# Two-block transformer kernel: the order of gate units around the first attention, and the place of one spread gate row

## The reference

```python
mod = c @ w_ada[l] + b_ada[l]
h = rmsnorm(x, norm_g[l]) * (1.0 + scale[:, None]) + shift[:, None]
qkv, z_attn, u_pool, z_pool, g_attn, g_pool = split(h @ w_in[l])
attn = sum_over_groups(softmax(lse) * attention(q, k, v, dilation, bias))
y_attn = (attn * silu(z_attn)) @ w_attn_br[l]
y_pool = (mixed_pool * silu(z_pool)) @ w_pool_br[l]
merged = sigmoid(g_attn) * y_attn + sigmoid(g_pool) * y_pool
x = x + gate[:, None] * (merged @ w_out[l])
```

```python
x = sublayer_residual(x, y, g1, ln_g[i, 0], ln_b[i, 0])
x = sublayer_residual(x, sq_relu_mlp(x * (1.0 + sc2) + sh2, w1[i], w2[i]), g2, ln_g[i, 1], ln_b[i, 1])
```

## Time and profile before

| | us |
|---|---|
| median of 3 runs | 1415.87 |
| lowest and highest | 1415.29, 1424.77 |
| the profiled execution | 1417.43 |
| its span in the profile | 1415.7 |
| PE busy | 1319.8 (93%) |
| DVE busy | 845.3 (60%) |
| ACT busy | 578.3 (41%) |
| POOL busy | 163.6 (12%) |

### The profile page before, as it was taken

How to read it: one execution, slowest core, us unless ns; L and a number is a source line. 1 busy time by engine, 2 the same in 40 slices (tenths; PEclk the granted TensorE clock), 3 DMA queues, 4 the chain that set the end, 5 groups by cost and what they waited for, 6 DMA issues and landing times.

```text
span 1415.7 us, 24506 instructions
## 1 busy us (share of the span) xinstructions
PE 1319.8 (93%) x10521; PEld 1216.9 (86%) x10521; DVE 845.3 (60%) x1265; ACT 578.3 (41%) x889; POOL 163.6 (12%) x167
## 2 busy tenths in 40 slices
PE   5999999999998999888999999999999998899995
PEld 2899988899887778778989898998999997899995
DVE  1867655565454355538765556655679875556663
ACT  2533345635753434414422313213254663434440
POOL 0111100000011111015400000000030121100002
PEclk8999999999999999999999999999999998899998
DMA  9987874545244543335444444434236003345550
GB/s 350 324 296 243 261 224 109 149 152 177 79 151 159 179 162 108 117 117 184 142 156 129 152 138 147 151 106 150 75 119 206 4 1 120 115 153 179 181 176 30
DMA packets 163593, 218.40 MB, mean 154 GB/s; under 512 B 5998, under 2 KB 141557, under 8 KB 163350
## 3 DMA queue, kind: packets, MB, share of 16 engines
q1 hardware_dynamic: 141060, 152.30, 32.8%
q0 software_dynamic: 21728, 63.23, 14.2%
q10 hardware_dynamic: 698, 1.32, 0.3%
HBM read 215.70 MB, written 1.12 MB: 153 GB/s over the span
## 4 chain that ended last, share of the span: by engine, by line
PE 76%; DVE 10%; ACT 5%; DMA 4%; issue 3%; POOL 1%; POOLq 0%; SPq 0%; DVEq 0%; ACTq 0%
PE bank L1301 29%; PE bank L701 11%; PE bank L718 10%; PE bank L751 6%; DVE wlo L2024 2%; PE bank L1377 2%; PE bank L812 2%; PE bank L734 2%; DMA graw_b<-in_w_mod 2%; DVE a_lo L2222 2%; PE bank L1392 2%; ACT whi L1454 1%; PE bank L1216 1%; PE bank L998 1%; PE bank L1145 1%
## 5 line engine op out<-in xcount | busy, mean ns | idle before, releaser
L2024 DVE TENSOR_TENSOR wlo<-raw,whi 128x2048 fp32r<-128x2048 f32 x131 | 299.3, 2286 | 129.3 <-ACT whi L1454 129.1
L1454 ACT ACTIVATE whi<-raw 128x2048 fp32r<-128x2048 f32 x131 | 248.6, 1900 | 223.9 <-PE bank L1301 150.9
L1301 PE MATMUL bank<-whi,m_hi 128*128 128x256 f32 x640 | 179.7, 281 | 10.2 <-DVE m_lo L2579 7.4
L1301 PE MATMUL bank<-wlo,m_hi 128*128 128x256 f32 x640 | 178.4, 279 | 0.0
L1301 PE MATMUL bank<-whi,m_lo 128*128 128x256 f32 x640 | 178.4, 279 | 0.0
L1301 PE MATMUL bank<-a_lo,whi 128*128 128x256 f32 (+1 forms) x448 | 148.5, 331 | 0.0
L1301 PE MATMUL bank<-a_hi,whi 128*128 128x256 f32 (+1 forms) x448 | 148.2, 331 | 0.0
L1301 PE MATMUL bank<-a_hi,wlo 128*128 128x256 f32 (+1 forms) x448 | 148.1, 331 | 0.0
L1301 PEld LDWEIGHTS bank<-whi,m_hi 128*128 128x128 f32 x640 | 121.9, 190 | 11.9 <-DVE m_lo L2579 8.6
L1301 PEld LDWEIGHTS bank<-wlo,m_hi 128*128 128x128 f32 x640 | 121.4, 190 | 0.1
L1301 PEld LDWEIGHTS bank<-whi,m_lo 128*128 128x128 f32 x640 | 121.3, 190 | 0.0
(11 more groups left out here) (398 smaller groups left out, 3242.8 us busy)
## 6 DMA issues: line engine op xcount, KB each, us to landing
raw<-in_mlp_w SPq DMA_DIRECT2D x64, 1024.0 KB, 5.1
graw_b<-in_w_mod POOLq DMA_DIRECT2D x80, 512.0 KB, 4.9
raw<-in_w_in SPq DMA_DIRECT2D x32, 1024.0 KB, 7.3
raw<-in_ev_w_in SPq DMA_DIRECT2D x12, 1024.0 KB, 5.1
pre<-in_w_ada SPq DMA_DIRECT2D x16, 512.0 KB, 10.6
graw_a<-in_w_mod POOLq DMA_DIRECT2D x16, 512.0 KB, 7.1
raw<-in_od_w_qkv SPq DMA_DIRECT2D x6, 1024.0 KB, 4.8
graw_a<-in_w_ada POOLq DMA_DIRECT2D x8, 512.0 KB, 6.7
```

The lines of the kernel that those rows point to most:

```text
L1301: mm = nc.tensor.matmul(o, x, y, start=(k == 0 and i == 0), stop=(k == KT - 1 and i == 2))
L1454: nc.scalar.activation(split_pair(u, kt * cols)[0], landing(u, kt * cols), ACT.Copy).then_inc(hi_done, 1)
L2024: nc.vector.tensor_tensor(split_pair(u, n)[1], landing(u, n), bf(whi[u % HI], n), ALU.subtract).then_inc(lo_done, 1)
```

## The change

The first attention begins with logits(0), the turn of vector block 9 and gate unit 24; after that each step n ends with gate unit 24+n+1, and the last step with none. For logits(0) and logits(1) PE waits for tiles 22 and 23 to be taken, in place of all tiles before logits(0). ACT copies the row of block 9 before it takes unit 23, and takes gate unit n's tile in step n. POOL issues the first strip_b when DVE's sums for the quarter before the last are done, and not when PE's last gemv is. In the second half gate row 6 is made in banks 6 and 7 before the output units and copied by ACT there, and PE waits for rowb_done before it transposes the normalised rows.

```diff
--- before.py
+++ after.py
@@ -408,7 +408,7 @@
         res_mul = sem("res_mul")
         RES = [0, 9, 13, 18, 22]
 
-        ROW_BANKS = {2: (0, 1), 3: (0, 1), 4: (4, 5, 6, 7), 5: (4, 5), 6: (4, 5)}
+        ROW_BANKS = {2: (0, 1), 3: (0, 1), 4: (4, 5, 6, 7), 5: (4, 5), 6: (6, 7)}
         TILES = 4
 
         def at_(v, r, per):
@@ -626,7 +626,7 @@
                 if h2:
                     pool.wait_ge(at_s, 4 * h2 - 1 + e)
                 elif e:
-                    pool.wait_ge(gemv_done, Q_B)
+                    pool.wait_ge(sum_step, sums_to(Q_B - 2))
                 pool.dma_start(strip[e][:, :, :, :],
                                bass.AP(tensor=parts.tensor, offset=parts.offset + h * 2 * GROUPS * 384,
                                        ap=[[1, P], [GROUPS * 384, 2], [384, GROUPS], [1, 256]])).then_inc(strip_full[e], 16)
@@ -941,15 +941,14 @@
 
             pe.wait_ge(mz_tmp, 2)
             pe.wait_ge(load_k, 16)
-            gemv_turn(9)
-            pe.wait_ge(mod_done, 10)
-            all_taken(pe, before[U_GATES])
             pe.wait_ge(anti_done, 1)
 
             def logits(n):
 
                 h2, qt = steps[n]
                 W = P * (qt + 1)
+                if n < 2:
+                    taken(pe, before[U_GATES] - 2 + n)
                 for e in range(2):
                     if n:
                         pe.wait_ge(at_p, 2 * n - 1 + e)
@@ -1000,6 +999,9 @@
                 mm.then_inc(at_pv, 1)
 
             logits(0)
+            gemv_turn(9)
+            col_unit(U_GATES, h_hi, h_lo, S, before[U_GATES])
+            pe.wait_ge(mod_done, 10)
             for n, (h2, qt) in enumerate(steps):
                 prob_transposes(n, 0, 0)
                 if n + 1 < len(steps):
@@ -1016,7 +1018,8 @@
                     prob_transposes(n, 1, 0)
                     values(n, 0, 0)
                     values(n, 1, 0)
-                col_unit(U_GATES + n, h_hi, h_lo, S, before[U_GATES + n])
+                if n + 1 < len(steps):
+                    col_unit(U_GATES + n + 1, h_hi, h_lo, S, before[U_GATES + n + 1])
             pe.wait_ge(mz_part, 2)
             col_unit(32, mz_hi, mz_lo, S, before[32])
             pe.wait_ge(at_z, 2 * len(steps))
@@ -1430,12 +1433,13 @@
                     window_values(n - 4)
                 if 2 <= n < PAIRS + 2:
                     window_turn(n - 2)
+            gate_rows((M1 + 40,), ROW_BANKS[6])
             pe.wait_ge(wa_o, PAIRS // 2)
             for u in range(U_OD, U_M1):
                 row_unit(u, o_hi, o_lo, range(NT), before[u])
+            pe.wait_ge(rowb_done, 6)
             turn_half(4, (0, 1))
             col_half(U_M1, 0, a_hi, a_lo, before[U_M1], t0=LN_T0[4])
-            gate_rows((M1 + 40,), ROW_BANKS[6])
             M1_ARGS = (U_M1, a_hi, a_lo, S, *half_m, 32, False)
             mlp(*M1_ARGS, range(1, 8), 0)
             for r in (1, 2, 3):
@@ -1508,6 +1512,8 @@
                 split_hi(u + LEAD)
                 if u and u % 4 == 0:
                     gemv_take(3 + u // 4)
+                if u == U_GATES - 1:
+                    gemv_take(9)
                 b = before[u]
                 src = take(b)[:, :].rearrange("p (m n) -> p m n", m=2)
                 if u < 2:
@@ -1533,8 +1539,6 @@
                         nc.scalar.activation(trA[g], bank[4 + g][:, :], ACT.Copy).then_inc(pool_ev, 1)
                     act.wait_ge(mz_tmp, 2)
                     nc.scalar.activation(flat(mz_hi), flat(u_row), ACT.Copy).then_inc(mz_part, 1)
-            gemv_take(9)
-
             def gate_unit(i):
                 b = before[U_GATES + i]
                 dst = gaT if i < 4 else gpT
@@ -1554,10 +1558,8 @@
                         last = nc.scalar.activation(prob[e][:, 2 * W:3 * W], bank[A_BANK[e][1]][:, 0:W], ACT.Exp,
                                                     bias=stat[:, c + 2:c + 3], accum_out=stat[:, c + 5:c + 6])
                     last.then_inc(at_p, 1)
-                if n:
-                    gate_unit(n - 1)
+                gate_unit(n)
                 split_hi(U_GATES + n + LEAD)
-            gate_unit(7)
             act.wait_ge(load_k, 16)
             split_hi(35)
             for i in range(2):
@@ -1994,11 +1996,11 @@
                     window_out((n - 6) // 2)
                 if n == PAIRS + 3:
                     take_rows(5)
+            take_rows(6)
             for u in range(U_OD, U_M1):
                 split_hi(u + LEAD)
             norm_part(4, 0, 2)
             affine_half(4, 0)
-            take_rows(6)
             for r in range(3):
                 mlp(U_M1, S, half_m[0], 32, r)
             mlp(U_M1, S, half_m[0], 32, 3, lead=8 - LEAD)
```

## The result

| | before | after |
|---|---|---|
| median, 4 runs each | 1416.15 | 1400.21 |
| lowest and highest | 1415.29, 1424.77 | 1397.39, 1400.93 |
| the profiled execution, and its span | 1417.43, 1415.7 | 1400.61, 1398.9 |

The ratio of the times is 0.987, with a 95% interval of 0.983 to 0.9911. The forecast was 1403.7 and "within 1%" the likeliest outcome; the kernel became 1.3% faster, and the number is that of rival 1 (1400.2). The same kernel measured again, beside the experiments (after_again), gave 0.9912 (0.9882 to 0.9942) with a median of 1404.51, which is near the forecast. So the gain is between 12 and 18 us, and the number alone does not choose between the forecast and rival 1; the traces do.

The account below looks back on a forecast made before the run. TensorE was taken as the bound, busy 1319.8 of 1415.7 us. Gains of 3.3 + 0 + 1.8 + 8.6 = 13.7 us from the profiled 1417.43 gave 1403.7, range 1400 to 1409.5.

Parts of the forecast that it names:

- rival 1: First attention: the strip wait goes altogether instead of moving; gain 17.2 us, to 1400.2; chance 0.17.
- (c): Attention steps: weight loads come one step earlier against strips, so logits(4)'s wait moves to logits(2); 0, bounds 3.5 either way.
- the clock at the start: Start of the attention: 3.6 us of pauses counted as covered, with no half-speed loss behind them priced.
- Start of the attention: From last row unit to gate unit 24: 3.6 us of pauses covered, less a 0.3 strip_b wait; gain 3.3 us.
- The pause ahead of the output units: Gate row fills PE's 1.7 us pause, so the clock does not fall behind it; gain 1.8 us.
- rival 2: Short pauses and their half-speed stretches: the clock gives less back; gain 10.5 us from the profiled time, taken as 1406; chance 0.22.
- Behind the layer norm: First MLP units: PE loses the row's 1.8 us, ScalarE starts hidden tiles sooner, m_lo wait falls to 0.8; gain 8.6 us.
- step 7 without a unit: Attention's last step: unit 32 follows at once and covers the scaling of za; nothing, 0.5 us if cover is short.
- the splits two steps ahead: Attention: splits run two steps ahead of PE rather than three, still over 10 us; cost nothing.
- the two copies ahead of the fourth output unit's split: Output units: ScalarE's row copies (1.09 us) precede a split needed three units (16 us) later; cost nothing.
- the wait for rowb_done: Before turn_half(4): PE's added wait was met four units earlier; cost nothing.
- The half-speed stretch in the layer norm: Layer norm, clock 0.50 from 1209.3 to 1212.4: it stays, perhaps ending 1.6 us sooner or later; taken as 0.

Follow-up runs that it names:

- load31_held: Kernel before, with SyncE holding unit 31's weight load until the strips for logits(4) landed; its group of four kernels measured ratios 0.9992 to 1.002.
- attn_only: Changed kernel with the gate row, its banks and its copy back in their old places; ratio 0.9961 against before.
- filled_pause: Kernel before plus 16 unread matmuls in PE's pause ahead of the output units; 1417.68 us, ratio 1.0001.
- row_twice: Changed kernel with PE making the gate row's 16 matmuls a second time in the old place, unread; 1405.54 us, ratio 0.9907 against before.
- copy_late: Kernel with only the attention edits, gate row made in its old place but copied by ScalarE only at MLP unit 4; 1403.79 us, ratio 0.9902 against before.
- row_only: Kernel before with only the gate row, its banks and its copy moved ahead of the output units; ratio 0.9925.

## Why the prediction was right or wrong

- **The failed step is (c): "The wait moves from one to the other: 0."** It went: 3.1 us in the trace, against the 3.5 that the step's bounds had. The reason given, weight loads of w_in in flight, was wrong (load31_held), and so was what followed from it, that the pair for logits(2) would take the wait over: its strip_b landed in 7.5 and cost 0.1. Every trace agrees: a wait of 1.3 to 1.9 at logits(4) in all eight with the units in their old places, and none above 0.3 there or at logits(2) in the six others. What makes that strip late stays open. Rival 1 had this outcome at 0.17. That its 1400.2 is the measured number to 0.1 us is luck, since the errors below cancel in part and after_again gave 1404.51.
- **A term at nothing beside it: the clock at the start.** The sum counted the pauses for the accumulator and the exp by their length, because in the one trace at hand no half-speed stretch followed them. In the seven other traces with the units in their old places one does, and costs an estimated 1.7 to 5.1 us there. The attention as a stage gains about 6 us, where the forecast had 3.3; how it divides between start and strip differs from execution to execution.
- **Start of the attention, 3.3:** 2.9 in the trace. The pauses for the accumulator and the exp are covered as worked out; strip_b landed in 8.40, with a wait of 0.7 where 0.3 was forecast, and 1.4 in the second execution. With step (c) the attention gives 6.0 in the trace and 5.5 by attn_only.
- **The pause ahead of the output units, 1.8:** nothing that filled_pause could show (its interval leaves room for it); the trace shows 0.3 up to the end of the first MLP unit. The term read one execution's half-speed stretch as a property of the kernel, and only two traces of seven have it. The doubt was in the text, but the sum kept the 1.9; by rival 2's own argument half or less was right.
- **Behind the layer norm, 8.6:** 8.1 in the trace. Its parts come out as well: 1.8 for the row on PE (row_twice, 1.8 forecast), and 6.2 for ScalarE's queue with the clock behind it (copy_late against attn_only, 6.8 forecast). The first square came at 1208.66, about 1.0 behind the end of PE's unit (0.9 forecast), the wait left is 0.8 as forecast, and no half-speed stretch follows it. This is the term that carries the change. The whole row part measures 10.6 (row_only), with 3 either way, against 8.6 and 1.8.
- **Costed at nothing:** step 7 without a unit, the splits two steps ahead, the two copies ahead of the fourth output unit's split, the wait for rowb_done. None of them shows among PE's waits of after. The half-speed stretch in the layer norm, priced at 0, is still there.
- **The chances.** The two misses have opposite signs (3.1 too little, 1.8 too much). The sum was 13.7, set against 1417.43; the gain by times is 5.5 + 10.6 = 16.1 from 1416.2. The forecast sat 2 us from the edge between "within 1%" and "faster", and 0.73 for the one side rested on step (c) being 0; with an unknown whose own bounds reached 3.5 either way, that was too firm. The second measurement (0.9912) lies at the same edge.

## What to carry to other kernels

An engine that is 41% busy can set the end: read what stands ahead of the critical copy in its in-order queue, and where a copy waits for a late producer, put it behind the work that others wait for, or make the producer earlier. A pause of under 2 us may have a half-speed stretch behind it in one execution and none in the next, so a forecast from one trace should count a stretch that it sees for less than it shows, and allow something for those that it does not see. Where the times of two kernels can't be told apart, compare the stage that was edited between the same two events in every trace: here the stage behind the layer norm repeats to 0.01 us in five traces, while the untouched stretch in the middle moves by 9 us. A transfer that is late by 1.5 us in one place of the program need not be late because of the large transfers that one sees beside it; hold them back once before pricing a step on that.

## What the runs showed of the hardware that was not expected

- A strip_b of 768 KB takes 6.9 to 7.6 us in most places behind the first, weight loads beside it or not, and 8.7 to 9.2 where a 16 KB fetch of instructions falls 4.75 to 6.25 us behind its issue. If the fetch is the cause, the order of instructions alone, far from the transfer, moves a wait in and out.
- At a granted clock of 1.00 a unit of 48 matmuls has two paces. The output tiles of before follow each other every 5.44 us; those of after every 5.65 us (below, 1169.50 being shown above), with the clock at 1.00. Of the fourteen traces, three (after, copy_late, load31_held) show 5.65 here and the others 5.44. With the half-speed stretches this makes executions differ where nothing was changed: from the transposes of za to the last window values they need 868.7 to 878.0 us. What sets the pace is not known.

```profile
1175.15 0.69 DVE L2441 TENSOR_TENSOR gtmp<-bank,Y 128x512 f32<-128x512 f32 x1 [1.25 <-PE bank L718]
1180.81 0.69 DVE L2441 TENSOR_TENSOR gtmp<-bank,Y 128x512 f32<-128x512 f32 x1 [1.26 <-PE bank L718]
1186.46 0.69 DVE L2441 TENSOR_TENSOR gtmp<-bank,Y 128x512 f32<-128x512 f32 x1 [1.25 <-PE bank L718]
```

- Where PE waited 1.8 us for the same strip in row_only, the clock behind the wait stayed at 1.00 (234.9 to 238.7 us); before, behind 1.9 us, it was 0.57.

```profile
234.90:238.70 3.80, 3.51 (x32) 3.28 (x33) 0.74 (x2) 1.78 (x2) 0.00 (x0) 1.00 0.64 250
```
